# One ones product of a group norm, moved behind the next application in a scan on one Trainium2 core

## The reference

```python
dt_f, dt_b = dt[..., :SSM_HEADS], dt[..., SSM_HEADS:]
a_neg = -jnp.exp(a_log.astype(jnp.float32))
y_f = ssd_chunked(xs, dt_f, a_neg[0], bm, cm)
y_b = flip(ssd_chunked(flip(xs), flip(dt_b), a_neg[1], flip(bm), flip(cm)))
y = (y_f + y_b).astype(x.dtype) + xs * d_skip[:, None]
y = y.reshape(bsz, t, SSM_D_INNER) * jax.nn.silu(z)
yg = y.astype(jnp.float32).reshape(bsz, t, SSM_GROUPS, SSM_D_INNER // SSM_GROUPS)
yg = yg * lax.rsqrt(jnp.mean(jnp.square(yg), -1, keepdims=True) + RMS_EPS)
y = yg.reshape(bsz, t, SSM_D_INNER).astype(x.dtype) * norm_w
return y @ w_out
```

## Time and profile before

| | us |
|---|---|
| median of 3 runs | 2308.41 |
| lowest and highest | 2307.0, 2309.49 |
| the profiled execution, its time | 2306.67 |
| its span in the trace | 2304.8 |
| TensorE busy | 2268.8 (98%) |
| VectorE busy | 978.4 (42%) |
| ScalarE busy | 445.5 (19%) |
| GpSimd busy | 74.0 (3%) |
| the scan's rounds 5 to 16, about | 506 to 572 from the span's start |

### The profile page before, as it was taken

The page is one execution under the profiler, slowest core; times in us unless marked ns, Lnnn a source line. Parts: engine busy times, 40 slices in busy tenths (PEclk is TensorE's granted clock), DMA queues, the critical chain, the costliest instruction groups (busy, mean ns, idle before and its releaser), DMA issues.

```text
span 2304.8 us, 25537 instructions
## 1 busy us (share of the span) xinstructions
PE 2268.8 (98%) x10774; PEld 1367.0 (59%) x10774; DVE 978.4 (42%) x1947; ACT 445.5 (19%) x1013; POOL 74.0 (3%) x130
## 2 busy tenths in 40 slices
PE   8999999999999999999999999999999999999998
PEld 5568547886487459997434333335999643333332
DVE  3567646668576557653211111125764311111122
ACT  3410003257100011220211211101132121111111
POOL 2000000000000000000000000000000000000000
PEclk9999999999999999999999999999999999999999
DMA  7279625454698415246999999994426599999997
GB/s 293 113 304 402 258 78 204 147 183 175 241 409 325 178 60 202 97 177 261 384 428 427 428 427 427 427 419 189 166 96 247 221 409 428 427 427 428 428 428 288
DMA packets 59167, 671.64 MB, mean 291 GB/s; under 512 B 7504, under 2 KB 7792, under 8 KB 18720
## 3 DMA queue, kind: packets, MB, share of 16 engines
q1 hardware_dynamic: 51888, 649.45, 69.1%
q0 software_dynamic: 7152, 20.43, 2.7%
HBM read 666.59 MB, written 3.26 MB: 291 GB/s over the span
## 4 chain that ended last, share of the span: by engine, by line
PE 87%; DMA 9%; DVE 2%; issue 0%; ACT 0%; SPq 0%; POOL 0%; DVEq 0%; POOLq 0%; ACTq 0%
PE ps L101 84%; DMA ring<-in_exp_w 6%; DMA arena<-in_exp_w 2%; DVE arena L114 1%; PE ps L349 1%; DVE arena L117 1%; PE ps L2736 1%; DMA arena<-ssm_rows 1%; DMA ring<-in_attn_w_in 0%; DMA ring<-in_ada_w 0%; PE ps L625 0%; PE ps L1898 0%; DVE X L117 0%; PE ps L1217 0%; ACT arena L106 0%
## 5 line engine op out<-in xcount | busy, mean ns | idle before, releaser
L101 PE MATMUL ps<-arena 128*64 128x512 f32 (+6 forms) x4020 | 952.3, 466 | 13.9 <-DMA arena<-in_exp_w 5.6
L101 PEld LDWEIGHTS ps<-arena 128*128 128x128 f32 (+2 forms) x4020 | 458.7, 167 | 463.8 <-issue 435.3
L101 PE MATMUL ps<-ring,arena 128*64 128x512 f32 (+2 forms) x1720 | 460.6, 584 | 2.1 <-DMA ring<-in_exp_w 2.1
L101 PE MATMUL ps<-XTGB,ring 128*128 128x256 f32 (+1 forms) x2160 | 423.5, 353 | 0.0
L101 PEld LDWEIGHTS ps<-XTGB,ring 128*128 128x128 f32 x2160 | 367.1, 190 | 52.8 <-issue 10.7
L101 PEld LDWEIGHTS ps<-ring,arena 128*64 128x64 f32 (+1 forms) x1720 | 174.4, 150 | 258.9 <-issue 254.7
L122 DVE COPY arena<-ps 128x512 f32<-128x512 f32 (+5 forms) x133 | 63.3, 496 | 417.3 <-PE ps L101 298.5
L121 ACT COPY arena<-ps 128x512 f32<-128x512 f32 (+3 forms) x179 | 81.6, 475 | 678.7 <-PE ps L2736 283.8
L101 PE MATMUL ps<-XTGB,arena 128*64 128x512 f32 (+2 forms) x736 | 200.7, 428 | 0.0
L105 ACT ACTIVATE arena<-ps 128x512 f32<-128x512 f32 (+2 forms) x95 | 51.2, 545 | 677.9 <-PE ps L101 673.0
L101 PE MATMUL ps<-ring,XTGB 128*128 128x512 f32 (+3 forms) x484 | 168.0, 501 | 1.6 <-DMA ring<-in_attn_w_in 1.4
(11 more groups left out here) (150 smaller groups left out, 954.0 us busy)
## 6 DMA issues: line engine op xcount, KB each, us to landing
arena<-in_exp_w SPq DMA_DIRECT2D x90, 2048.0 KB, 26.3
ring<-in_exp_w SPq DMA_DIRECT2D x68, 2048.0 KB, 27.7
ring<-in_mlp_w SPq DMA_DIRECT2D x25, 2048.0 KB, 9.2
ring<-in_ada_w SPq DMA_DIRECT2D x20, 2048.0 KB, 9.7
XTGB<-in_exp_w SPq DMA_DIRECT2D x18, 2048.0 KB, 32.0
ring<-in_ssm_w_in SPq DMA_DIRECT2D x12, 2048.0 KB, 7.8
ring<-in_w_in SPq DMA_DIRECT2D x12, 2048.0 KB, 7.9
ring<-in_gate_w SPq DMA_DIRECT2D x12, 2048.0 KB, 7.9
```

Source lines behind the costliest of these rows:

```text
L101: return self.e.matmul(o, lhsT=lhsT, rhs=rhs, start=start, stop=stop, skip_group_check=True)
```

## The change

The instructions are the same; their places in the lists change.
- TensorE: the ones products of groups 0 to 5 move from the end of the even round 2g + 4 to the odd round 2g + 5, behind the application and ahead of the z or output product. Groups 6 and 7 stay.
- ScalarE: Ln and Exp of groups 0 to 5 move from round 2g + 4 to round 2g + 5, behind that round's Exps and ahead of `z_out`, `z_silu` and `squares`. Groups 6 and 7 stay.
- VectorE: the last multiplies of groups 0 to 5 move from round 2g + 5 to 2g + 7, those of groups 6 and 7 from rounds 17 and 19 to 18 and 20.

```diff
@@ ssm_pe
                 if i in (SP, SP + 2):
                     norm_b((i - 4) // 2)
+                elif 5 <= i < SP and i % 2 == 1:
+                    norm_b((i - 5) // 2)
                 if i < 12:
                     z_chunk(pe, 4 + i)
...
-                if 4 <= i < SP and i % 2 == 0:
-                    norm_b((i - 4) // 2)
@@ ssm_act
-                if i >= 4 and i % 2 == 0 and (i - 4) // 2 < 8:
+                if i in (SP, SP + 2):
                     norm_b((i - 4) // 2)
+                elif 5 <= i < SP and i % 2 == 1:
+                    norm_b((i - 5) // 2)
@@ ssm_dve
-                if i >= 5 and i % 2 == 1 and (i - 5) // 2 < 8:
-                    norm_c((i - 5) // 2)
+                if 7 <= i < SP + 2 and i % 2 == 1:
+                    norm_c((i - 7) // 2)
+                if i in (SP + 2, SP + 4):
+                    norm_c((i - 6) // 2)
```

## The result

The changed kernel takes 2315.02 us (median of 8 runs, 2310.3 to 2317.93) against 2309.0 us before (median of 8, 2307.0 to 2309.92). The ratio is 1.0028, with a 95% interval of 1.0019 to 1.0037: 6.0 us slower, where 6.0 were forecast. The profiled execution took 2316.43 us, its span is 2314.6.

What follows compares the result with a forecast made beforehand. TensorE was taken as nearly full, waiting before odd applications on VectorE's list and ScalarE's square. Shifts grew from +1.27 us at round 7 to +4.73 at round 15 and +5.96 at group 6's product: 2308.4 + 6.0 = 2314.4 us, range 2310.4 to 2318.0.

Steps and rivals of the forecast that it cites:

- two feeders: Scan, ahead of odd rounds' applications: VectorE's list, begun when a row load lands, and ScalarE's square end TensorE's waits.
- Part 1, the ones products: TensorE, scan: six ones products pass behind the next application; 0 to 0.5 us each, 3.0 at most, no separate term.
- the not-slower rival: Scan: ScalarE's square is not last, as with one table load per block; only 3.0 us paid, 2311.4; chance 0.2.
- Part 2, the block ahead of the square: ScalarE, odd rounds: the 3.40 us block delays the square; Exps to application 9.53 us in ordinary rounds, 11.90 in silu rounds.
- Round 15 to group 6's product: Scan's end: round 15's Exps at 571.76, group 6's ones product at 578.03 against 572.07, +5.96 us.
- Part 3, VectorE's multiplies: VectorE: last multiplies one pair of rounds later, hidden, cost 0; 0.9 us if the cover were gone.
- The late row load: Rounds 9 and 13: row load taken to land in 6.5 us, not the median 4.3, setting the applications of 11 and 15.
- Nothing gives it back: Behind the scan: weight loads wait for ring places that TensorE frees later by the same amount; the +6.0 us stays.
- The signs in the profile: Scan: square begins 5.1 to 8.4 us after its Exps; TensorE idles 1.5 to 2 us before rounds 7, 9, 13.
- faster: Scan: block hidden, VectorE's shorter list sets the start; 3 to 4 us gained at best, near 2305; chance 0.05.
- Self-feeding: Scan: later applications delay row loads three rounds on, terms add further; 10.5 us, 2319; chance 0.1.
- The clock: TensorE, scan: longer waits drop its clock; one pair of rounds at 1.2 GHz adds up to 11.6 us, 2326; chance 0.03.

Runs made afterwards that it cites:

- ScalarE's cured alone: Kernel before, with ScalarE's square ahead of the z copy and silu in odd rounds: 2308.71 us, ratio 0.9999.
- both cured: Kernel before, square ahead of z copy and silu, last multiplies of groups 0 to 5 in even rounds behind the skip: 2307.02 us, 0.9991; again 2307.68, 0.9993.
- the two pairs of traces named with the result: Stretch's end to span's end: two traces of the changed kernel, 1719.2 and 1717.9 us; two of another kernel, 1719.2 and 1717.1.
- block last: Changed kernel with ScalarE's block of groups 0 to 5 as last step of the odd round, behind copy, silu and square: 2308.95 us, ratio 1.0001.
- block without loads: Changed kernel with Square in place of the norm's Ln, so both table loads of each block go: stretch 82.69 us, total time not read.
- the longer block: Changed kernel with two more ScalarE copies of 128 x 436 behind the norm's Exp in rounds 5, 7, 9, 11, 13: 2319.81 us, ratio 1.0048.
- the square first: Changed kernel with ScalarE's square ahead of the silu in rounds 3, 7, 11, block still ahead of the square: 2316.84 us, ratio 1.0034.

## Why the prediction was right

- **What bounds it** (two feeders, ScalarE without reserve in a silu round): right. The experiments add that the two take turns and that VectorE's hides ScalarE's: ScalarE's cured alone brought nothing, both cured 1.9 to 2.0 us. VectorE's cured alone was not run, so that it too would bring nothing is not shown.
- **Part 1, the ones products** (0 to 0.5 us each, no term of its own beside ScalarE's): right in kind. Undoing this part alone gives back 0.5 in all. The bound of 3.0, which was also the price of the not-slower rival, was far too high: with the block out of the square's way 0.6 and 0.7 us were measured (block last, block without loads). The working had charged all six products, but ahead of rounds 7, 11 and 15 these kernels have no wait, and the product fills time that a wait had taken. It also said only that the z product behind the ones product has no wait of its own, and not that ScalarE's z copy waits for the z product in a silu round; by that way each of the pairs from round 7 to 9 and from 11 to 13 is 0.35 longer with the block last than before.
- **Part 2, the block ahead of the square**: right, and shown: 5.2 of 5.8 us go when only the block's place in the round changes, and 5.1 when its table loads go. The two chain lengths, 9.53 and 11.90, can be read as 520.44 − 510.99 = 9.45 (round 5's Exps to round 7's application) and 533.66 − 521.86 = 11.80. Two terms are a little too long. Weighing to application is 2.07 (518.37 to 520.44) instead of 2.15, which had been read where a ones product stood directly ahead of the application; with TensorE's part undone, where it stands there again, it is 2.15 (518.73 to 520.88). And round 7's Exps follow the weighing's start by 3.49 (518.37 to 521.86), not 3.65. Together they make most of the 0.14 by which the forecast is late at round 7, and of the 0.55 at round 15.
- **Round 15 to group 6's product**, a miss of the other sign: forecast 7.77 (570.26 to 578.03), measured 8.16 (570.85 to 579.01). The sum let round 15's Exps follow its application by 1.50; they follow by 1.91 (572.76), because the least step waits 0.39 for a row load that took only 3.92 to land. The end figure, 5.96 against 5.80, is therefore closer than the terms in it: that 0.4 of the 0.55 cancels is luck.
- **Part 3, VectorE's multiplies**: right, cost 0 (stretch 81.93 with this part alone).
- **The late row load** (6.5 instead of 4.3 in rounds 9 and 13): right, 6.49 in round 9 and 6.4 in round 13. Round 11's idle of 0.57 is what it cost.
- **Round 16** (group 6's product about 1 us late, ahead of output products that do not need it): right, 1.12.
- **Nothing gives it back**: right up to 830 us, 6.92 of 6.95. The sign of being wrong that the prediction names, another time from 578 to the end, did occur, with 2.9 us, but this is of the size by which traces of one kernel differ there (1.3 and 2.1 in the two pairs of traces named with the result).
- **The signs in the profile**: VectorE's norm sum waits for ScalarE in all even rounds from 6 on, as said. The square begins 5.4 us behind its round's Exps in round 5 (516.37 and 510.99) and 7.7 in round 7; the 8.4 of the prediction is where it ends there (8.36). The wait ahead of round 7 is 1.34 instead of 1.5 to 2; those ahead of 9 and 13 fit.
- **The rivals**: the one by which Ln and Exp share a load did not occur, the loads stood at 1.28 each before both. That a short enough block costs little is shown by the kernel without loads; a block with one load, which is that rival's case, was not run. In "faster" the 1.35 are five waits, not six; the sixth, ahead of round 5, is 0.34 more. "Self-feeding" did not go beyond the terms of the sum. The clock did not fall in either trace of the changed kernel; it did once in each of the two kernels whose waits were longer, at 1.6 us each and not 11.6.

## What to carry to other kernels

Where an engine is full and waits a little in each round, write down which other engine ends each wait, in every kind of round, before moving anything: where two feeders take turns, curing one can bring nothing while curing both pays, as it did here for ScalarE's. A block may be moved to a round where its engine has time and still cost, if it lands ahead of the one small step that the next engine waits for; put what is urgent first in a round and what is free last. A small product on the full engine costs the same in front of a neighbour or behind it, as long as the neighbour's operand is ready; but look also at who waits for what now comes behind it.

## What the runs showed of the hardware that was not expected

- TensorE's granted clock fell to 0.50 for about 3 us (546 to 549 in one trace, 563 to 566 in the other) within a stage in which it was otherwise 1.00, after an idle of 2.23 us in the first and 2.71 in the second, and cost 1.6 us each time. Idles of 2.57 (with the longer block) and of 2.01 (with the square first, ahead of round 7, where the pair kept its 11.50 us of work) passed without it. What decides between them is open.
- In the thirteen row loads of each trace that wait for an application, a load of 512 KB lands in 3.7 to 4.4 us or in 6.2 to 6.6, and which it is repeats by round: the long ones are those that rounds 5, 9 and 13 wait for, in all fourteen traces. In the trace of before they are issued at 502.28, 525.97 and 549.62, and a weight slab of 2 MB is issued 2.6 us ahead of each (499.7, 523.4, 547.0) and takes 8 us to land. The two thus overlap in time; that the slab is what slows the row load is argued from this, no run took the slab away.
